# Constant tiles multiplied on TensorE in its waits between the stages of an encoder layer

## The chip, the cores and the metric
One core of one Trainium2 chip. The metric is the device time of one execution in microseconds (us); lower is better. TensorE is the matrix engine, VectorE, ScalarE and GpSimd compute on rows, SyncE issues DMAs.

## The reference
One encoder layer on 1536 tokens (a prompt of 512 and a sample of 1024) of width 1024, in f32:
```
h    = rmsnorm(x, g_mix);  proj = h @ w_in              # 1024 -> 2496 columns
ret  = retention_bidir(rope(q), rope(k), v)              # 8 heads of 64, chunks of 128
mla  = latent_attention(cq, ckv, kr)                     # 4 heads, ranks 256 and 128
x    = x + concat(gated ret, mla) @ w_out
h    = rmsnorm(x, g_ffn)                                 # router: 4 groups x 8 experts,
y    = sum over top-2 of gate * (silu(h@w_g[e]) * (h@w_u[e])) @ w_d[e]
out  = rmsnorm(x + y, g_final)
```
Each expert (32 of them) has three matrices of 1024x512 in f32, 6 MB.

## The kernel before
It runs as stages, each with its own instruction stream per engine; semaphores order the engines. A large product is made by `three_passes` (lines 94 to 98): operands are split into a high and a low part of type fp32r, and hi x hi, hi x lo and lo x hi are added in PSUM. Router, transposes and a few small products are plain f32.

**Projection** (`phase_project`, TensorE from line 338). The loop over 12 token tiles runs twice: V and K first, then Q, C (the latent part) and G, with scores and outputs of the retention between them. At its end TensorE does `turn(N - 2)`, `outputs(N - 1)`, then `turn(N - 1)`: four transposes that wait for GpSimd's gated row (line 320). ScalarE copies the result (line 591), GpSimd stores it (line 324), and the stage ends in a barrier of all engines, after which the semaphores are cleared (lines 105 to 107).

**Attention** (`phase_latent`, TensorE from line 1258). Weights are absorbed first: 8 groups of three 128x128 products into `pt`, after `w_lo` of VectorE (line 1582). Then comes a wait for the constants `s_const` (identity and rotary angles, both loaded by SyncE, lines 1051 and 1053), then `values(0)` (four transposes, waiting for GpSimd's `key_lo` of four tiles, line 1090), `values(1)`, `rotary`, `queries`, and a loop over 48 units of 128 query rows. The last `weigh_last(1)` goes to ScalarE (line 1382) and to memory, and the stage ends in a barrier.

**Mixing and routing** (`phase_mix`, TensorE from line 1870). `project(t, half)` makes 48 matmuls of 128x512 for one tile. For tile t, TensorE issues in this order: `project(t + 1)`, `match_places(t - 2)`, a wait for `x2` (VectorE line 2026), 8 transposes (line 1906), `place_in_queue(t - 1)` (lines 1887 and 1888), a wait for ScalarE's copies of the transposes (line 1942), and the router's 8 matmuls of 36 columns (line 1915). VectorE takes `x2`, the reciprocal root (line 2028), the normalised row (line 2030), the queue steps of the tile before (`queue`, lines 1984 to 2018; the first is line 1988), and the choice of experts (lines 2037 to 2060). In the last tile (`last`), ScalarE does its two copies ahead of the square root (lines 1949 to 1952). After the loop: `match_places(10)`, `place_in_queue(11)`, `match_places(11)`, then the matmul that counts rows per expert (line 1925). VectorE's last steps write `ex.first` (line 2068), the list of the rows of expert 0; it then splits two weight pieces (line 2070).

**Experts** (`phase_experts`, TensorE from line 2322), in the same block, so without a barrier. GpSimd gathers the rows of expert 0 (line 2221) by `ex.first`. TensorE waits for them, transposes them (line 2326), ScalarE and VectorE split them into `xT_hi` and `xT_lo` (line 2472), and `take_in` and `give_out` make the expert's products. Weights come as six pieces of 1 MB per expert into six buffers; a piece is loaded when VectorE has split the one before in its buffer (`s_wlo`, lines 1716 and 2165). VectorE's first expert step is `rows_lo(0)`, two splits and `count_blocks`. All engines execute their instructions in program order.

Of the kernel before, what the change touches and what calls it, by code (L numbers as in the profile page):

```python
# [28 lines left out]
P = 128  # L29
# [64 lines left out]
def three_passes(pe, out, st_hi, st_lo, mv_hi, mv_lo, first, last):  # L94

    pe.matmul(out, st_hi, mv_hi, start=first, stop=False)  # L96
    pe.matmul(out, st_hi, mv_lo, start=False, stop=False)  # L97
    return pe.matmul(out, st_lo, mv_hi, start=False, stop=last)  # L98


def phase_sems(nc, ctx):
# [16 lines left out]
def phase_project(nc, x_all, w_in, g_mix, g_q, g_kv, rope, ident_d, log_decay, gn_g, dist_d, index_d, span_d, mid, mixT, w_cat, absorb, shared):  # L118
    with ExitStack() as ctx:
# [30 lines left out]
        ident = sb("ident", [P, P])  # L150
# [187 lines left out]
        def _(pe):  # L338
# [69 lines left out]
            def turn(t):  # L408
                pe.wait_ge(s_ret, t + 1)
                pe.wait_ge(s_ctev, min(t + 2, N))  # L410
                if t == N - 1:
                    pe.wait_ge(s_rtev, t)
                for j in range(4):
                    ins = pe.transpose(pT[:, j * P:(j + 1) * P], o_sb[:, j * P:(j + 1) * P], ident[:])
                ins.then_inc(s_rt, 1)
# [81 lines left out]
                turn_latent(t)  # L497
            turn(N - 2)
            outputs(N - 1)
            turn(N - 1)  # L500

        @block.scalar
        def _(act):
# [420 lines left out]
def out_piece(shared, table, k, c):  # L924

    first = table[k][c] * 512
    return shared[:, first:first + 512]


def phase_latent(nc, mid, w_cat, w_out, rope, ident_d, mixT, absorb, shared):  # L930

    SCALE = float(NOPE + ROPE) ** -0.5
    with ExitStack() as ctx:
# [8 lines left out]
        ident = sb("ident", [P, P])  # L942
# [151 lines left out]
        def _(pe):  # L1094
# [153 lines left out]
            def aside(u):  # L1248
# [6 lines left out]
                elif u == 44:  # L1255
                    fold(3, 1)

            pe.wait_ge(s_wlo, 1)
            for h in range(HM):
                for k in range(2):  # L1260
# [4 lines left out]
                if h % 2 == 1:  # L1265
                    ins.then_inc(s_m, 1)
            pe.wait_ge(s_const, 32)
            values(0)
            values(1)
            rotary(0)  # L1270
# [9 lines left out]
            for u in range(NU):  # L1280
# [12 lines left out]
                if u == NU - 2:  # L1293
                    weigh_last(0)
            weigh_last(1)

        @block.scalar
        def _(act):
# [421 lines left out]
def phase_mix(nc, block, sems, shared, split, plain, acc, ex, mixT, x_all, g_ffn, w_rg, w_re, ident_d, route_d, blocks_d, x_mid,  # L1720
              h_rows, table, s_tick, s_tock, w_exp):
    with ExitStack() as ctx:
# [43 lines left out]
        pt = acc[:, 2048:3072]  # L1766
# [101 lines left out]
        @block.tensor  # L1868
        def _(pe):
            def project(t, half):  # L1870
                pe.wait_ge(s_mlo, t + 1)
                pe.wait_ge(s_x2, t - 1 if not isinstance(t, int) else max(0, t - 1))
                for b in range(2):
                    for k in range(KD):
                        rows = slice(k * P, (k + 1) * P)
                        ins = three_passes(pe, po[half][:, b * 512:(b + 1) * 512], mT_hi[:, half, rows],
                                           mT_lo[:, half, rows], out_piece(shared, OUT_HI, k, b),
                                           out_piece(shared, OUT_LO, k, b), k == 0, k == KD - 1)
                ins.then_inc(s_po, 1)

            project(0, 0)
            pe.wait_ge(s_const, 112)

            def place_in_queue(t):

                pe.wait_ge(s_hot, t + 1)
                pe.matmul(pp[:, 0:NE], before, hot[:, 2, :], start=True, stop=False)
                pe.matmul(pp[:, 0:NE], ones, seen[:], start=False, stop=True).then_inc(s_pp, 1)

            def match_places(t):  # L1890

                pe.wait_ge(s_match, t + 1)
                pe.matmul(pp[:, 64:65], match[:], row_id[:], start=True, stop=True).then_inc(s_matched, 1)

            def tile(r, half, last):
                t = 2 * r + half
                if not last:
                    project(t + 1, 1 - half)
                if not (isinstance(r, int) and r == 0):
                    match_places(t - 2)  # L1900
                pe.wait_ge(s_x2, t + 1)
                pe.wait_ge(s_htev, 2 * t)
                for b in range(2):
                    for j in range(4):
                        k = 4 * b + j
                        ins = pe.transpose(pt[:, k * P:(k + 1) * P], x2[:, half, k:D:KD], ident[:])  # L1906
                    ins.then_inc(s_ht, 1)
                if not (isinstance(t, int) and t == 0):
                    place_in_queue(t - 1)
                pe.wait_ge(s_htev, 2 * t + 2)  # L1910
                pe.wait_ge(s_rev, t)
                if isinstance(t, int) and t == 0:
                    pe.wait_ge(s_wr, 1)
                for k in range(KD):
                    ins = pe.matmul(pr[:, 0:NG + NE], hT[:, k * P:(k + 1) * P], w_r[:, k, :],  # L1915
                                    start=k == 0, stop=k == KD - 1)
                ins.then_inc(s_r, 1)

            pairs(pe, TILES, tile)
            match_places(TILES - 2)  # L1920
            place_in_queue(TILES - 1)
            match_places(TILES - 1)
            pe.wait_ge(s_spot, TILES + 1)
            pe.wait_ge(ex.s_first, 1)
            pe.matmul(pp[:, 0:NE], ones, seen[:], start=True, stop=True).then_inc(s_count, 1)
# [174 lines left out]
def phase_experts(nc, block, sems, split, plain, acc, ex, w_exp, h_rows, table, s_tick, x_mid, g_final, out, s_normed, count_blocks,  # L2100
# [4 lines left out]
    with ExitStack() as ctx:  # L2105
# [216 lines left out]
        def _(pe):  # L2322
# [30 lines left out]
            def turn_hidden(n):  # L2353
# [3 lines left out]
                    ins = pe.transpose(ph[:, k * P:(k + 1) * P], h_sb[:, k:FE:KF], ident[:])  # L2357
                ins.then_inc(s_ht, 1)

            pe.wait_ge(s_xg[0], 16)  # L2360
            transpose_rows(0, 0)
            transpose_rows(1, 0)

            def step(r, half, final):
                n = 2 * r + half
# [283 lines left out]
```

## Time and profile before

| | us |
|---|---|
| median of 3 runs | 1635.18 (1634.63 to 1635.73) |
| the profiled execution, its own time | 1637.01 |
| its span, first to last instruction | 1635.5 |
| busy: TensorE / VectorE / ScalarE / GpSimd | 1488.1 / 1102.0 / 876.5 / 283.6 |
| mean granted TensorE clock | 0.957 of full |

The profile's page shows busy time by engine and the span in 40 slices of 41 us, with the granted TensorE clock of each. The trace behind it has every instruction with its start, its duration and what ended the idle time before it. Tables of stretches give, after the length, busy us and number of records of TensorE's matmuls, TensorE's weight loads, VectorE, ScalarE and GpSimd, then the granted clock, the DMA engines' busy share and GB/s. A granted clock of 1.00 is 2.4 GHz and 0.50 is 1.2 GHz. A matmul's duration holds its way through the array and overlaps the next; what a row of matmuls costs is the distance between starts.

### The profile page before, as it was taken

To read this page: it belongs to the slowest core of one execution; us is meant where nothing else is said; L and a number is where in the kernel's file an instruction comes from. 1 tells how busy PE (TensorE), PEld (TensorE's weight loads), DVE (VectorE), ACT (ScalarE), POOL (GpSimd) and SP (SyncE) were. 2 spreads that over 40 slices of the span, in tenths; PEclk is the share of its full clock that TensorE was granted. 3 is DMA by queue.
4 is the path that set the end of the run, shared out by engine and by line. 5 is a ranking of instruction groups with operands and counts; after the bars stand their busy time and mean duration, and the time that the engine had idled before them with its cause. 6 is when DMAs were issued, how large, how long until landed. Compare 5 with 4: busy or idle time off the path is not lost.

```text
span 1635.5 us, 21860 instructions
## 1 busy us (share of the span) xinstructions
PE 1488.1 (91%) x7520; PEld 1246.9 (76%) x7520; DVE 1102.0 (67%) x1649; ACT 876.5 (54%) x1150; POOL 283.6 (17%) x270
## 2 busy tenths in 40 slices
PE   6999999999994889998799985999999999999992
PEld 5888888888884677777688874878887878788771
DVE  5655765344343666666256657988888888888886
ACT  6434433233233554554243444867777777777764
POOL 0000111111112300000012123432122212123341
PEclk9999999999996899999899986999999999999996
DMA  7222421221112110001653425999999999999997
GB/s 244 71 95 95 142 69 59 85 71 59 52 39 86 39 59 20 26 29 37 217 215 134 154 80 191 368 377 376 386 381 384 382 366 383 384 384 383 378 346 268
DMA packets 79175, 323.62 MB, mean 198 GB/s; under 512 B 13574, under 2 KB 23814, under 8 KB 54530
## 3 DMA queue, kind: packets, MB, share of 16 engines
q1 hardware_dynamic: 62418, 274.63, 44.7%
q0 software_dynamic: 16688, 48.10, 9.6%
q8 instruction: 40, 0.66, 0.2%
q14 instruction: 29, 0.24, 0.0%
HBM read 279.62 MB, written 51.80 MB: 203 GB/s over the span
## 4 chain that ended last, share of the span: by engine, by line
DMA 19%; PE 13%; DVE 10%; issue 5%; ACT 3%; POOL 1%; ACTq 0%; DVEq 0%; SPq 0%; POOLq 0%
DMA plain<-in_w_down 17%; DVE split L1716 7%; PE acc L96 4%; PE acc L98 4%; PE acc L97 4%; DMA plain<-s_h_rows,plain 1%; PE acc L1915 1%; ACT split L2418 1%; ACT shared L1710 1%; PE acc L1906 1%; DVE plain L2528 1%; DVE shared L1716 0%; POOL s_x_mid L2230 0%; ACT plain L1942 0%; PE acc L2326 0%
## 5 line engine op out<-in xcount | busy, mean ns | idle before, releaser
L1710 ACT CAST shared<-plain 128x2048 fp32r<-128x2048 f32 x192 | 364.8, 1914 | 99.5 <-DMA plain<-in_w_up 67.5
L96 PE MATMUL acc<-shared,split 128*128 128x512 f32 x960 | 386.1, 402 | 20.3 <-DVE split L1969 9.7
L98 PE MATMUL acc<-shared,split 128*128 128x512 f32 x960 | 378.9, 395 | 0.0
L1716 DVE TENSOR_TENSOR split<-plain,shared 128x2048 fp32r<-128x2048 f32 x128 | 287.3, 2285 | 0.0
L96 PEld LDWEIGHTS acc<-shared,split 128*128 128x128 f32 x960 | 183.7, 191 | 58.6 <-DVE split L1969 9.9
L98 PEld LDWEIGHTS acc<-shared,split 128*128 128x128 f32 x960 | 182.9, 190 | 39.6
L97 PE MATMUL acc<-split 128*128 128x512 f32 x512 | 200.7, 392 | 0.0
L96 PE MATMUL a_p<-shared,a_xT_hi 128*128 128x512 f32 (+1 forms) x480 | 194.8, 406 | 3.3 <-DVE a_w_lo L690 3.3
L98 PE MATMUL a_p<-shared,a_xT_lo 128*128 128x512 f32 (+1 forms) x480 | 187.3, 390 | 0.0
L97 PE MATMUL acc<-shared,split 128*128 128x512 f32 x448 | 177.7, 397 | 0.0
L1716 DVE TENSOR_TENSOR shared<-plain,shared 128x2048 fp32r<-128x2048 f32 x64 | 146.0, 2282 | 4.0 <-ACT shared L1710 4.0
L2230 POOL DMA_INDIRECT s_x_mid<-plain x30 | 56.2, 1873 | 384.1 <-DVE plain L2479 379.2
L97 PEld LDWEIGHTS acc<-split 128*128 128x128 f32 x512 | 97.2, 190 | 18.4
L97 PE MATMUL a_p<-a_w_lo,a_xT_hi 128*128 128x512 f32 (+1 forms) x288 | 110.8, 385 | 0.0
L96 PEld LDWEIGHTS a_p<-shared,a_xT_hi 128*128 128x128 f32 x480 | 91.4, 190 | 20.2 <-DVE a_xT_lo L684 3.7
L98 PEld LDWEIGHTS a_p<-shared,a_xT_lo 128*128 128x128 f32 x480 | 91.1, 190 | 18.0
L97 PEld LDWEIGHTS acc<-shared,split 128*128 128x128 f32 x448 | 86.4, 193 | 18.1
L1374 ACT CAST c_pT_hi<-c_pt 128x512 fp32r<-128x512 f32 x80 | 45.2, 589 | 76.2 <-PE c_pt L1207 76.1
L2221 POOL DMA_INDIRECT plain<-s_h_rows,plain x32 | 78.0, 2437 | 19.9 <-PE acc L2326 6.5
L97 PE MATMUL a_p<-shared,a_xT_hi 128*128 128x512 f32 x192 | 75.5, 393 | 0.0
L802 DVE TENSOR_TENSOR a_late<-a_p,a_dmat 128x512 f32<-128x512 f32 x24 | 16.6, 691 | 85.1 <-PE a_p L388 85.1
L1545 DVE TENSOR_TENSOR c_pT_lo<-c_pt,c_pT_hi 128x512 fp32r<-128x512 f32 x80 | 52.7, 684 | 22.9 <-ACT c_pT_hi L1374 22.9
(349 smaller groups left out, 2617.1 us busy)
## 6 DMA issues: line engine op xcount, KB each, us to landing
plain<-in_w_gate SPq DMA_DIRECT2D x64, 1024.0 KB, 11.1
plain<-in_w_up SPq DMA_DIRECT2D x64, 1024.0 KB
plain<-in_w_down SPq DMA_DIRECT2D x64, 1024.0 KB, 10.8
a_x_sb<-in_x SPq DMA_DIRECT2D x24, 512.0 KB, 4.2
s_mid<-a_kv SPq DMA_DIRECT2D x12, 512.0 KB, 2.9
a_kv<-s_mid SPq DMA_DIRECT2D x12, 512.0 KB, 3.5
plain<-s_mixT SPq DMA_DIRECT2D x12, 512.0 KB, 5.4
plain<-in_x SPq DMA_DIRECT2D x12, 512.0 KB, 4.0
```

The costliest lines, as they stand in the source:

```text
L96: pe.matmul(out, st_hi, mv_hi, start=first, stop=False)
L97: pe.matmul(out, st_hi, mv_lo, start=False, stop=False)
L98: return pe.matmul(out, st_lo, mv_hi, start=False, stop=last)
L802: nc.vector.tensor_tensor(sc[:, odd].rearrange("p a i -> p (a i)"), pS[:], dmat[:, odd].rearrange("p a i -> p (a i)"), ALU.mult).then_inc( ...
L1374: nc.scalar.copy(pT3_hi[:, 4 * i:4 * i + 4, j * P:(j + 1) * P], pt[:, c * 512:(c + 1) * 512].rearrange("p (k i) -> p k i", k=4)).then_inc( ...
L1545: nc.vector.tensor_tensor(pT3_lo[:, 4 * i:4 * i + 4, j * P:(j + 1) * P], pt[:, c * 512:(c + 1) * 512].rearrange("p (k i) -> p k i", k=4), ...
L1710: eng.copy(self.w_hi[j // 2][:, cols], self.source(j, moved)).then_inc(self.s_whi[j], 1)
L1716: eng.tensor_tensor(self.w_lo[j // 2][:, cols], self.source(j, moved), self.w_hi[j // 2][:, cols].bitcast(F32), ALU.subtract).then_inc(sel ...
L1906: ins = pe.transpose(pt[:, k * P:(k + 1) * P], x2[:, half, k:D:KD], ident[:])
L1915: ins = pe.matmul(pr[:, 0:NG + NE], hT[:, k * P:(k + 1) * P], w_r[:, k, :], start=k == 0, stop=k == KD - 1)
L2221: pool.indirect_dma_start(out=xg[half][:], out_offset=None, in_=h_rows, in_offset=bass.IndirectOffsetOnAxis(ap=index, axis=0), bounds_chec ...
L2230: pool.indirect_dma_start(out=x_rows, out_offset=bass.IndirectOffsetOnAxis(ap=index, axis=0), in_=y_sb[half][:], in_offset=None, bounds_ch ...
```

## The change
A helper issues `times` matmuls of a constant tile by a constant tile into a PSUM region that nobody reads before it is overwritten. It is called at twelve places of TensorE's stream: 102 matmuls of 128x512 fp32r (16, 28, 12, 12, 14 and 20) and 140 of the f32 identity by itself, 128x128 (36, 32, 6, 7, 52 and 7). No wait is added or removed, and no other engine's stream is changed.
```diff
--- before.py
+++ after.py
@@ -96,6 +96,12 @@
     pe.matmul(out, st_hi, mv_hi, start=first, stop=False)
     pe.matmul(out, st_hi, mv_lo, start=False, stop=False)
     return pe.matmul(out, st_lo, mv_hi, start=False, stop=last)
+
+
+def keep_warm(pe, out, weights, moving, times):
+
+    for _ in range(times):
+        pe.matmul(out, weights, moving, start=True, stop=True)
 
 
 def phase_sems(nc, ctx):
@@ -497,7 +503,10 @@
                 turn_latent(t)
             turn(N - 2)
             outputs(N - 1)
+            spare = w_lo[0][:, 2, :]
+            keep_warm(pe, bank[0][:], spare[:, 0:P], spare, 16)
             turn(N - 1)
+            keep_warm(pe, bank[0][:], spare[:, 0:P], spare, 28)
 
         @block.scalar
         def _(act):
@@ -1255,6 +1264,8 @@
                 elif u == 44:
                     fold(3, 1)
 
+            spare = shared[:, 13312:13824]
+            keep_warm(pe, pt[:, 0:512], spare[:, 0:P], spare, 12)
             pe.wait_ge(s_wlo, 1)
             for h in range(HM):
                 for k in range(2):
@@ -1265,6 +1276,7 @@
                 if h % 2 == 1:
                     ins.then_inc(s_m, 1)
             pe.wait_ge(s_const, 32)
+            keep_warm(pe, ps[0][:, 0:512], spare[:, 0:P], spare, 12)
             values(0)
             values(1)
             rotary(0)
@@ -1293,6 +1305,8 @@
                 if u == NU - 2:
                     weigh_last(0)
             weigh_last(1)
+            spare = v_hi[:, 0:4, :].rearrange("p t d -> p (t d)")
+            keep_warm(pe, ps[0][:, 0:512], spare[:, 0:P], spare, 14)
 
         @block.scalar
         def _(act):
@@ -1878,6 +1892,8 @@
                                            out_piece(shared, OUT_LO, k, b), k == 0, k == KD - 1)
                 ins.then_inc(s_po, 1)
 
+            spare = out_piece(shared, OUT_HI, 0, 0)
+            keep_warm(pe, po[1][:, 0:512], spare[:, 0:P], spare, 20)
             project(0, 0)
             pe.wait_ge(s_const, 112)
 
@@ -1898,6 +1914,8 @@
                     project(t + 1, 1 - half)
                 if not (isinstance(r, int) and r == 0):
                     match_places(t - 2)
+                if last:
+                    keep_warm(pe, po[0][:, 0:P], ident[:], ident[:], 36)
                 pe.wait_ge(s_x2, t + 1)
                 pe.wait_ge(s_htev, 2 * t)
                 for b in range(2):
@@ -1918,8 +1936,11 @@
 
             pairs(pe, TILES, tile)
             match_places(TILES - 2)
+            keep_warm(pe, po[0][:, 0:P], ident[:], ident[:], 32)
             place_in_queue(TILES - 1)
+            keep_warm(pe, po[0][:, 0:P], ident[:], ident[:], 6)
             match_places(TILES - 1)
+            keep_warm(pe, po[0][:, 0:P], ident[:], ident[:], 7)
             pe.wait_ge(s_spot, TILES + 1)
             pe.wait_ge(ex.s_first, 1)
             pe.matmul(pp[:, 0:NE], ones, seen[:], start=True, stop=True).then_inc(s_count, 1)
@@ -2357,9 +2378,11 @@
                     ins = pe.transpose(ph[:, k * P:(k + 1) * P], h_sb[:, k:FE:KF], ident[:])
                 ins.then_inc(s_ht, 1)
 
+            keep_warm(pe, py[:, 0:P], ident[:], ident[:], 52)
             pe.wait_ge(s_xg[0], 16)
             transpose_rows(0, 0)
             transpose_rows(1, 0)
+            keep_warm(pe, py[:, 0:P], ident[:], ident[:], 7)
 
             def step(r, half, final):
                 n = 2 * r + half
```

## Rows read from the trace of the kernel before

**Rows 1.** The page: busy time and record count of each engine; granted clock by slices.
```profile
PE 1488.1 (91%) x7520; PEld 1246.9 (76%) x7520; DVE 1102.0 (67%) x1649; ACT 876.5 (54%) x1150; POOL 283.6 (17%) x270
...
PEclk9999999999996899999899986999999999999996
```

**Rows 2.** Table of stretches (from:to, length; each engine busy us and records; clock; DMA).
```profile
480.00:490.60 10.60, 9.83 (x69) 8.46 (x68) 2.38 (x4) 3.06 (x4) 3.49 (x3) 1.00 0.14 51
...
494.00:521.00 27.00, 10.84 (x47) 10.00 (x48) 6.70 (x8) 7.43 (x15) 8.72 (x14) 0.50 0.43 129
...
507.70:512.90 5.20, 5.14 (x24) 5.14 (x24) 1.73 (x4) 3.58 (x9) 4.12 (x7) 0.50 1.04 296
...
784.00:794.00 10.00, 3.90 (x9) 3.13 (x10) 1.23 (x1) 1.04 (x1) 1.95 (x8) 0.50 0.80 237
...
968.80:971.60 2.80, 0.01 (x1) 0.00 (x0) 2.02 (x14) 0.00 (x0) 1.57 (x2) 1.00 0.01 0
...
971.90:1005.70 33.80, 15.07 (x55) 13.15 (x56) 21.13 (x70) 15.23 (x16) 9.30 (x10) 0.50 0.37 126
...
974.00:980.30 6.30, 6.25 (x28) 6.02 (x28) 1.92 (x7) 5.18 (x7) 0.57 (x1) 0.50 0.21 83
...
1040.00:1560.00 520.00, 506.28 (x2355) 416.94 (x2354) 458.52 (x309) 385.89 (x308) 144.36 (x94) 1.00 1.01 380
```

**Rows 3.** Timeline of TensorE, 477 to 520 us (start, us; bracket: idle before).
```profile
495.44 1.12 PE L414 MATMUL a_p<-a_ident,a_late 128*128 128x128 f32 x4 [4.60 <-POOL a_late L320]
...
516.66 1.09 PE L1108 MATMUL c_po<-c_ident,c_key_hi 128*128 128x128 f32 x4 [3.52 <-POOL c_key_lo L1090]
```

**Rows 4.** Timeline of TensorE, start of the mixing.
```profile
790.10 0.79 PE L96 MATMUL acc<-shared,split 128*128 128x512 f32 x1 [9.69 <-DVE split L1969]
```

**Rows 5.** Timeline of TensorE, 952 to 1020 us, the routing tail.
```profile
966.64 1.98 PE L1915 MATMUL acc<-plain 128*128 128x36 f32 x16 [0.35 <-ACT plain L1942]
...
968.45 0.36 PE L1893 MATMUL acc<-plain 128*128 128x1 f32 x2
...
974.05 1.97 PE L1906 MATMUL acc<-plain 128*128 128x128 f32 x8 [5.24 <-DVE plain L2026]
...
980.72 0.58 PE L1893 MATMUL acc<-plain 128*128 128x1 f32 x2 [0.39 <-DVE plain L1997]
...
986.09 0.63 PE L1887 MATMUL acc<-plain 128*128 128x32 f32 x2 [4.79 <-DVE plain L2058]
...
988.23 0.59 PE L1893 MATMUL acc<-plain 128*128 128x1 f32 x2 [1.08 <-DVE plain L1997]
...
998.35 1.97 PE L2326 MATMUL acc<-plain 128*128 128x128 f32 x8 [7.58 <-DMA plain<-s_h_rows,plain]
...
1001.72 0.79 PE L96 MATMUL acc<-shared,split 128*128 128x512 f32 x1 [1.40 <-DVE split L2472]
```

**Rows 6.** Timeline of TensorE at 480 us.
```profile
479.60 0.39 PE L97 MATMUL a_p<-shared,a_xT_hi 128*128 128x512 f32 x1
479.83 0.39 PE L98 MATMUL a_p<-shared,a_xT_lo 128*128 128x512 f32 x1
480.15 1.16 PE L388 MATMUL a_p<-a_qd,a_kv 64*128 64x128 f32 x8
```

**Rows 7.** Groups of TensorE by line and shape: the router's matmul.
```profile
L1915 PE MATMUL acc<-plain 128*128 128x36 f32 x192 | 25.4, 291 | 4.2 <-ACT plain L1942 4.2
```

**Rows 8.** Instructions of line 119: duration min/median/max ns, start us.
```profile
L119 POOLq DRAIN  x1: 2997/2997/2997, 500.0 to 500.0; - x1
```

**Rows 9.** Timeline of SyncE at 506 us, and DMA issues there (last: us to landing).
```profile
506.45 0.57 SPq L1053 DMA_DIRECT2D c_angles<-in_rope  x1
...
c_angles<-in_rope SPq DMA_DIRECT2D x1, 768.0 KB, 7.1
```

**Rows 10.** Timeline of VectorE in the tail.
```profile
978.28 0.17 DVE L2028 RECIPROCAL plain<-plain 128x1 f32<-128x1 f32 x1 [4.29 <-ACT plain L1952]
...
987.19 0.16 DVE L1988 COPY plain<-acc 128x1 f32<-128x1 f32 x1 [0.95 <-PE acc L1888]
```

## The prediction

> **What bounds the kernel now.** First the page: TensorE is busy for 91% of the span, and its granted clock is high except in a few slices; every matmul record has a weight load of its own, 7520 against 7520 [rows 1]. Then the table of stretches, which gives the clock level and the records of each: three stretches at 1.2 GHz (clock 0.50) matter, 494.0 to 521.0, 784.0 to 794.0 and 971.9 to 1005.7; from 1040 to 1560 the DMA engines are full and TensorE has 506 of 520 us of work [rows 2]. So the end is set by one thread: projection, attention and mixing on TensorE and its partners, then the routing tail (967 to 1002), then weights that stream at the DMA limit. The stream begins when the expert stage begins, so a microsecond won or lost before 1002 reaches the end nearly whole. The waits that the change fills are 4.6 us before the last turn of the projection, the barrier after it, 3.5 us before values(0) [rows 3], 9.7 us ahead of the mixing [rows 4], and in the tail 5.2, 4.8, 1.1 and 7.6 us [rows 5]. Each ends on another engine or a DMA: if the filler is longer than the wait, TensorE is what is late.
>
> **Prices.** The change adds 102 matmuls of 128x512 fp32r and 140 of ident by ident, plain f32. The first kind starts every 0.23 us at the high clock (479.60 to 479.83) [rows 6], and costs 0.43 at the low one (9 records in 3.90) [rows 2]. The second is the point. A plain f32 matmul leaves two records: the router has 8 matmuls in each of 12 tiles and shows 192 [rows 7]. Sixteen such records run from 966.64 to 968.45, 0.113 each [rows 5]; with 128 moving columns, as ident has, eight take 1.16 us, start-up and last end included, 0.145 each [rows 6]. I take 0.112 a record, 0.224 a matmul, since the second figure holds both ends. At the low clock 24 records of 128x128 take 5.14 us, 0.213 each [rows 2], so 0.427 a matmul. Identical weights one after another would not be loaded once only: loads equal matmuls everywhere [rows 1].
>
> The Trainium skill, page "TensorE: Matmul & The Clock Gate", section "Back-to-back issue gap", gives about 81 ns for a sustained matmul of 128 columns with its load. By that figure alone (an estimate) 36 would take 2.9 us and 52 would take 4.2 us, and all fillers would fit.
>
> **End of the projection.** 16 matmuls are 3.6 us of a 4.6 us wait; the turn then runs at the high clock and its 1.12 us [rows 3] shrink by about 0.45. It is on the path (ScalarE copy, store, barrier): -0.45. The 28 behind it are 6.4 us, done near 502.5. GpSimd is in a drain of 3.0 us from 500.0 to 503.0 ahead of the barrier [rows 8], which hides them: 0, but with 0.1 us to spare, and were that cover gone they would cost up to 2 us.
>
> **Start of attention.** 12 matmuls (2.7 us) fit between the barrier at 504 and the products of the absorbed weights at 507.7 [rows 2], and those 24 go faster, to no use: values(0) at 516.66 waits for GpSimd's key_lo, not for them [rows 3]. The next 12 stand behind a wait for the constants, which includes the angles: issued 506.45, 7.1 us to landing, so 513.5 [rows 9]. From the products' end near 510 to 513 TensorE idles 3 us; in this kernel 2.8 us (968.8 to 971.6) without work is followed by the low clock [rows 2]. So they probably begin low and end between 515.8 (all high, hidden) and 518.2 (all low, values(0) 1.5 late); I take 0.6 late. The clock is then high from values(0) on instead of from 521: what ran 516.66 to 521.0 at half speed takes about 2.3 us less, less 0.4 where ScalarE's eviction decides. Sum: -1.3 (between -2.3 and 0). A later wait of this stage that the change does not fill may drop the clock as now or at another moment: 0, up to 1.5 either way.
>
> **Start of the mixing.** 14 (3.2 us) behind the last weighing end by 783.6, before the barrier; 20 (4.5 us) from 784.5 end by 789.1, before the first projection at 790.10 [rows 4]. That one then runs 9 matmuls at 0.23 instead of 0.43: -1.9. Nothing hides it: the tiles of the mixing follow on TensorE one behind the other. In all the front gives -0.45 - 1.3 - 1.9 = -3.6; the level may dip elsewhere too, once the work has moved (a tile of the mixing dips when its router work falls badly), so I take -3.2, between -6 and 0.
>
> **The routing tail**, times as before, the front's gain left out. (a) 36 ident matmuls are queued at 968.67, ahead of the wait for x2: 72 x 0.112 = 8.05, to 976.7, where the transposes had started at 974.05 [rows 5]. Behind them are ScalarE's two copies and its square root, then VectorE's reciprocal at 978.28, 4.23 after the transposes' start [rows 10]; fast transposes make that about 3.35, so 980.05: +1.8. (b) match_places(10) moves to 982.5. Before it lies the router's 36-column work and a wait of 2 us, much like what preceded 971.9, so I hold the clock to be low again near here. Then 32 matmuls: 64 x 0.213 = 13.7, to 996.6, where place_in_queue(11) wanted to start at 986.09 + 1.8 = 987.9. VectorE's next step, 1.10 behind it (986.09, 987.19) [rows 5, 10], comes at 997.6: +10.4. (c) 6 matmuls, 2.6 us, fill a wait that is 1.1: with the delay so far +10.7. (d) ex.first and the gather follow, rows landing at 998.35 + 10.7 = 1009.05; 7 and then 52 matmuls, 14 and 104 records, 25.2 us with the count's matmul between, hold TensorE until 1026.0: +27.7. (e) 7 more after the transposes, 3.0 us, against a wait of 1.4 (1000.3 to 1001.72): +29.0. VectorE's splits of weights and the count of blocks stand behind xT_lo, and the buffers that free the next loads behind those; so VectorE, TensorE and the stream all start late. Nothing there can move forward. Total +29.0 - 3.2 = +25.8.
>
> Why the fillers should not bring the clock back themselves: the 24 records of 128x128 at 507.7 to 512.9 had 5.14 of 5.2 us and stayed at 1.2 GHz; so did the 28 records of 974.0 to 980.3 (6.25 of 6.3 us) [rows 2]. These are the rows nearest to ident by ident. What did raise it were 512-column records, after 3.9 us of them from 790.10 [rows 2, 4].
>
> The skill's page says the reverse as advice (section "Why this matters for your kernels": keep TensorE busy continuously to reach and hold the high clock). By that rule the second rival below comes out. Its section "Part 4: PE-mode transpose" says that transposes do not bring the full clock; 974.0 to 980.3 agrees.
>
> The profiled execution took 1637.01 us (span 1635.5), so the sum is 1662.8 in its terms; the median of the runs is 1.83 lower: **1661.0 us**.
>
> **Rivals.** A, forecast: clock low from (b) to the experts: 1661, and 1655 to 1670 with its unknowns (drop late in (b): -3; the front; and if (a) already falls low, 36 x 0.427 = 15.4 instead of 8.05: +7.4). Chance 0.62.
> B, the ident matmuls hold or raise the clock. For: the fillers leave little idle, and short f32 records at the high level kept it (480.0 to 490.6 is at 1.00 throughout [rows 2]). Against: the two stretches above. All high: (a) +1.8, (b) 989.9 against 987.9 and less 0.5 for the faster pair: +3.3, 52 x 0.224 = 11.6 puts the transposes at 1005.5, +7.2; the faster transposes and first expert products give back 2.8: about +4.4 on TensorE, but VectorE's chain begins +6.4 late and is full to 1040. So +6.4 - 3.2 = +3.2, 1638.4; with one low spell of 16 records, 2 us more, 1640.4. Chance 0.28.
> C, the other side: faster. If ident by ident costs one record, the 36 take 4.0 us of 5.2, the 52 take 5.8 of 7.6, nothing is late and all is high: tail -0.3 - 0.5 - 0.8 - 1.9 = -3.5, sum -6.8, 1628.4. It decides at 0.146 us a matmul (5.24/36; 7.58/52). For: the counts fill three quarters of each wait at 0.112. Against: two records in every f32 matmul. Chance 0.06.
> D, the clock does what B says and the front gives its full 6: 1634 to 1637, chance 0.04.
>
> **Numbers.** The likeliest case gives 1661. The range must reach into B: 1637 to 1670 leaves out C, D and the far end of A, under 2 in 10; A's own is 1655 to 1670. About 0.2% (3.3 us) is what a measurement of this kernel can tell from no change. Faster by more, C: 0.08 with a strong front. Within: B's lower half and D: 0.12. Slower: 0.80.
>
> **What would show it.** The page: 382 more matmul records (102 + 280). Table of stretches: 784 to 814 at 1.00 and 516 to 521 mostly so; in the tail 0.50 from about 982 to the experts, ident records 0.213 apart, the 52 taking 22 us, and idle time of TensorE before place_in_queue(11) and the first gather's transposes gone, with VectorE waiting for TensorE instead. If those records are 0.11 apart, B is right; if there are 140 of them, C. If the transposes do not start late at (a), the sum fails at its first step.

## The result, and the profile after

The changed kernel is slower: 1645.97 us median (8 runs, 1642.03 to 1652.84) against 1637.72 (8 runs, 1634.63 to 1641.85) of the kernel before beside it, ratio 1.0047, interval 1.003 to 1.0063. The forecast was 1661.0. The profiled execution took 1646.24 us (span 1644.7), 9.2 more than the 1637.01 of before. In the changed kernel the filler's line is L104, L388 to L420 of before are 6 lines further down, and L1887 to L1925 have become L1903 to L1946.

The page, answering to [rows 1]:
```profile
PE 1536.8 (93%) x7902; PEld 1290.4 (78%) x7902; DVE 1101.5 (67%) x1649; ACT 875.8 (53%) x1150; POOL 289.4 (18%) x270
...
PEclk9999999999999999999999999999999999999996
```
382 more matmul records, so ident by ident does leave two records each. The three dents of the clock line before (68, 8 and 86) are gone, and the time goes up all the same.

Table of stretches of the changed kernel (columns as in [rows 2]; the third from the end is the granted clock):
```profile
512.00:517.00 5.00, 4.69 (x15) 3.63 (x16) 0.70 (x2) 1.21 (x3) 2.38 (x5) 0.66 0.29 100
517.00:521.00 4.00, 3.67 (x26) 3.22 (x25) 1.86 (x4) 0.58 (x1) 0.00 (x0) 1.00 0.24 66
784.00:794.00 10.00, 9.20 (x41) 7.25 (x40) 1.23 (x1) 1.05 (x1) 1.17 (x6) 1.00 0.78 236
969.70:974.10 4.40, 4.40 (x26) 4.40 (x26) 3.48 (x22) 0.14 (x1) 2.01 (x2) 0.61 0.01 0
...
985.70:991.00 5.30, 5.30 (x26) 5.30 (x27) 4.06 (x26) 0.18 (x2) 2.15 (x3) 0.50 0.51 179
991.00:999.30 8.30, 8.30 (x76) 8.30 (x75) 2.90 (x20) 7.22 (x5) 0.00 (x0) 0.99 0.00 0
999.30:1011.00 11.70, 11.70 (x107) 11.70 (x107) 4.02 (x3) 0.00 (x0) 5.01 (x3) 1.00 0.57 207
...
1040.00:1560.00 520.00, 506.61 (x2367) 417.32 (x2366) 459.51 (x309) 390.05 (x311) 146.27 (x91) 1.00 1.01 381
```
The rows of the tail decide. The 72 records of the first group begin at 969.7. The first eight start 0.11 us apart, at the high level, then come sixteen 0.21 apart (0.61 over 969.7 to 974.1), then 0.11 again: the clock fell and rose inside one unbroken group. From 985.7 to 991 TensorE works through ident by ident at 0.50, and from 991 on, still in the same 64 records, at 0.99: here the clock rose inside the fillers. From 999.3 to 1011 there is nothing but fillers, at 1.00. And the stream from 1040 to 1560 is as it was, so what the tail loses stays lost.

Timeline of TensorE in the routing tail, answering to [rows 5]:
```profile
969.51 0.36 PE L1909 MATMUL acc<-plain 128*128 128x1 f32 x2
969.74 9.91 PE L104 MATMUL acc<-plain 128*128 128x128 f32 x72
979.49 1.04 PE L1924 MATMUL acc<-plain 128*128 128x128 f32 x8
...
985.27 0.58 PE L1909 MATMUL acc<-plain 128*128 128x1 f32 x2 [2.05 <-DVE plain L2018]
985.72 9.96 PE L104 MATMUL acc<-plain 128*128 128x128 f32 x64
995.52 0.31 PE L1903 MATMUL acc<-plain 128*128 128x32 f32 x2
...
999.28 11.86 PE L104 MATMUL acc<-plain 128*128 128x128 f32 x104
1010.97 1.04 PE L2347 MATMUL acc<-plain 128*128 128x128 f32 x8
```
Each group is longer than the wait that it fills (5.2, 4.8 and 7.6 us before). The steps behind the fillers have no bracket any more: nothing outside TensorE holds them up. VectorE now waits for TensorE instead. Timeline of VectorE, answering to [rows 10] (the reciprocal, and the first step behind place_in_queue(11)):
```profile
982.84 0.16 DVE L2049 RECIPROCAL plain<-plain 128x1 f32<-128x1 f32 x1 [7.78 <-ACT plain L1973]
...
996.09 0.16 DVE L2009 COPY plain<-acc 128x1 f32<-128x1 f32 x1 [5.30 <-PE acc L1904]
```
Timeline of TensorE at the two front places, answering to [rows 3, 4]:
```profile
494.51 0.66 PE L420 MATMUL a_p<-a_ident,a_late 128*128 128x128 f32 x4 [0.89 <-POOL a_late L326]
494.93 6.63 PE L104 MATMUL a_p<-shared 128*128 128x512 f32 x28
...
512.31 4.61 PE L104 MATMUL c_ps<-shared 128*128 128x512 f32 x12 [3.04 <-DMA c_angles<-in_rope]
516.75 0.60 PE L1117 MATMUL c_po<-c_ident,c_key_hi 128*128 128x128 f32 x4
...
783.25 4.78 PE L104 MATMUL acc<-shared 128*128 128x512 f32 x20 [1.00 <-PEq L113]
788.83 0.50 PE L96 MATMUL acc<-shared,split 128*128 128x512 f32 x1 [0.80 <-DVE split L1990]
```

Where the 9.2 us come from, as differences of the same instruction's start in the two traces, each counted from the first transpose of its execution:

| instruction | change minus before, us |
|---|---|
| VectorE's x2 of tile 0 of the mixing | -3.24 |
| x2 of tile 11 | +1.02 |
| first transpose of tile 11 | +5.39 |
| place_in_queue(11) | +9.38 |
| `ex.first` | +8.85 |
| first transpose of the first gathered rows | +12.57 |
| transposes of the second gather | +10.57 |
| end | +9.19 |

Not all of the first row is the fillers' doing. The last turn of the projection, whose start is set by GpSimd and not by a filler, already stands 0.98 us earlier (495.44 less 4.94 for the first transpose before, 494.51 less 4.99 after), and so does VectorE's work from 200 us on, long before the first filler. So the front's fillers bring 2.3 us, the mixing takes 4.3, the tail costs 11.55, and 2.0 of that come back because the experts' first products run at 2.4 GHz.

The mixing was in no step of the change. Its stretch 800 to 965, before, then the change:
```profile
800.00:965.00 165.00, 161.11 (x839) 137.46 (x838) 91.96 (x374) 65.20 (x94) 30.68 (x40) 0.98 0.46 166
```
```profile
800.00:965.00 165.00, 159.98 (x818) 136.22 (x817) 91.92 (x374) 65.10 (x94) 30.10 (x39) 0.96 0.46 166
```
The clock drops for a few microseconds on single tiles, twice before and four times here. Each of the 41 drops of this stretch in the fifteen profiles of this case begins inside the router's 36-column matmuls or within 1.1 us of the start of their last record. A drop costs 1.3 to 1.7 us, most 1.6 (steps in the distances between the x2 of neighbouring tiles). Only one of before's two cost anything: tile 2 took 16.65 us with its drop, and 16.60 without one in the run with fp32r fillers in the tail.

### The profile page after: what moved, and what is told of

It reads as the page before. It is cut to its first block, busy times and chain, and to the rows that moved or that the text cites. A ratio compares the mean times of both kernels' runs of the same rounds, so it can differ in the third digit from the quotient of the medians.

```text
span 1644.7 us, 22623 instructions
## 1 busy us (share of the span) xinstructions
PE 1536.8 (93%) x7902; PEld 1290.4 (78%) x7902; DVE 1101.5 (67%) x1649; ACT 875.8 (53%) x1150; POOL 289.4 (18%) x270
## 4 chain that ended last, share of the span: by engine, by line
DMA 21%; PE 13%; DVE 10%; issue 5%; ACT 3%; SPq 0%; ACTq 0%; DVEq 0%; POOLq 0%; POOL 0%
DMA plain<-in_w_down 18%; DVE split L1730 8%; PE acc L96 3%; PE acc L98 3%; PE acc L97 3%; PE acc L104 2%; DMA plain<-s_mixT 1%; PE acc L1933 1%; ACT split L2441 1%; ACT shared L1724 1%; DVE plain L2551 1%; DMA s_x_mid<-plain 1%; PE acc L1924 1%; ACT plain L1963 0%; DMA plain<-s_x_mid 0%
## 5 line engine op out<-in xcount | busy, mean ns | idle before, releaser
L2242 POOL DMA_INDIRECT plain<-s_h_rows,plain x32 | 85.6, 2673 | 24.6 <-DVE plain L2089 9.9
```

The source lines that it names most:

```text
L2242: pool.indirect_dma_start(out=xg[half][:], out_offset=None, in_=h_rows, in_offset=bass.IndirectOffsetOnAxis(ap=index, axis=0), bounds_chec ...
```

## The experiments

Differences "at x2 of tile 0", "at x2 of tile 11", "at the gathered rows" and "at the end" are measured as in the table above. They hold what the execution had won or lost before the first filler: at the projection's last turn the profiles of the runs stand between -0.62 and +2.59 us. The kernel before took 1639.37 us (32 runs), 1638.52 (23 runs), 1639.14 (23 runs) and 1639.16 (7 runs) beside the four groups of runs.

**Front alone.** All ident calls left out:
```diff
-                    keep_warm(pe, po[0][:, 0:P], ident[:], ident[:], 36)
...
-            keep_warm(pe, py[:, 0:P], ident[:], ident[:], 7)
```


> Edit: the six fillers of identity tiles in the routing tail are left out; the six of 128x512 fp32r stay. Theory Q (queue): the loss comes from identity tiles that are queued ahead of real work and outlast the waits, 2 records of 0.11 us each. Then this kernel keeps the front's gain (the first x2 of the mixing 3.2 us earlier than before) and has the tail of before: 3 us faster than before, ratio 0.998, less what low spells in the mixing tiles take. Rival L (level): the loss comes from moving the work against the clock's low spells, which fall on mixing tiles (4.3 us given back there in the changed kernel). Then this kernel is no faster than before, 1.000 to 1.001, with four low spells in the mixing.


Measured: 1642.39 us, ratio 1.0011 (0.9996 to 1.0025). In its profile x2 of tile 0 stands at -2.2 us (0.4 of that from before the first filler) and tile 11 at +1.0: 3.2 us go in the mixing. One of its two drops, from 830.6 to 837.4, lasts twice as long as the others. The time is what rival L gave, with two drops and not four.

**Tail alone.** The six fp32r calls left out:
```diff
-            keep_warm(pe, bank[0][:], spare[:, 0:P], spare, 16)
...
-            keep_warm(pe, po[1][:, 0:512], spare[:, 0:P], spare, 20)
```


> Edit: only the six fillers of identity tiles in the routing tail, none of the six of 128x512. Theory Q: the transposes of expert 0's rows start 11 us later than before and the experts' later blocks 9 to 10 us, ratio 1.006. Rival L: 1.000 to 1.002, since nothing ahead of the tail has moved.


Measured: 1646.9 us, ratio 1.0046 (1.0029 to 1.0064). The ident fillers carry the whole slowdown. From x2 of tile 11 to the gathered rows the tail is 11.0 us longer (expected 11; the change: 11.55), and 2.7 come back before the second gather.

**Half the ident counts**, front kept:
```diff
-                    keep_warm(pe, po[0][:, 0:P], ident[:], ident[:], 36)
+                    keep_warm(pe, po[0][:, 0:P], ident[:], ident[:], 18)
...
-            keep_warm(pe, py[:, 0:P], ident[:], ident[:], 52)
+            keep_warm(pe, py[:, 0:P], ident[:], ident[:], 26)
```
(32 became 16, 6 and both 7 became 3.)


> Edit: as the change, but the identity fillers halved: 18, 16, 3, 3, 26 and 3, so that at 0.224 us a tile each ends before its wait does (4.0 of 5.2, 3.6 of 4.8, 0.7 of 1.1, 5.8 of 7.6). Theory Q: no delay in the tail, the transposes of expert 0's rows about 1 us early and the first expert products 2 us shorter, so 3 to 6 us faster than before, ratio 0.997. If the clock falls in the tail in spite of them, the 26 tiles take 11 us at the low level and come 3 us late: about 1.000. Rival L: 1.000 to 1.003, as the change nearly.


Measured: 1637.81 us, ratio 0.9999 (0.9979 to 1.0018). x2 of tile 11 to the gathered rows: -0.2 against before. At two records a matmul, counts of half the size fit into the waits, as the 0.224 us of a matmul say (18 x 0.224 = 4.0 of 5.2; 26 x 0.224 = 5.8 of 7.6), and 1.9 us come back in the experts' first products. The 3 to 6 us that theory Q expected did not come: this profile stands at +0.1 at tile 0, and, with two drops, at +2.1 at tile 11.

**Only the 52 halved:**
```diff
-            keep_warm(pe, py[:, 0:P], ident[:], ident[:], 52)
+            keep_warm(pe, py[:, 0:P], ident[:], ident[:], 26)
```


> Edit: the change with 26 identity tiles instead of 52 ahead of the wait for expert 0's rows. Theory Q: the rows land near 1007.3 in the changed kernel's time while the 52 tiles end at 1011.0, so this one is 3.7 us faster than the changed kernel, ratio to before 1.0025. Rival (the gather is what is late, and the tiles are hidden beside it): as the changed kernel, 1.005.


Measured: 1647.36 us, ratio 1.0044 (1.0025 to 1.0064). Timeline of TensorE at this place:
```profile
1000.53 6.05 PE L104 MATMUL acc<-plain 128*128 128x128 f32 x52
1008.42 1.51 PE L2347 MATMUL acc<-plain 128*128 128x128 f32 x8 [1.83 <-DMA plain<-s_h_rows,plain]
```
The wait for the gather is back: 26 end before the rows land, so in the change 52 made TensorE 12.57 - 8.85 = 3.7 us late. The runs' median does not show these 3.7 us: it lies between the 1.0025 of theory Q and the 1.005 of its rival. In this profile the clock dropped five times in the mixing and x2 of tile 11 stands at +4.2, which hides them (from there to the gathered rows it is 5.8 us, against 11.55); whether that holds for all 12 runs (1637.82 to 1653.8) is not shown.

**512-column fillers in every tile of the mixing**, none of the change's:
```diff
                 if not (isinstance(t, int) and t == 0):
                     place_in_queue(t - 1)
+                keep_warm(pe, po[half][:, 0:512], spare[:, 0:P], spare, 2)
                 pe.wait_ge(s_htev, 2 * t + 2)
```


> The kernel before, with none of the change's fillers, and 2 fillers of 128x512 fp32r in each of the 12 tiles of the mixing, between the pair of place_in_queue of the tile before and TensorE's wait for s_htev. So far the mixing showed 2, 4, 2, 6, 2 and 6 spells at the low clock in the profiled executions of six kernels. Theory L (those spells set how far the front's gain is given back, about 1.7 us each): with 512-column records in TensorE's wait of each tile the spells between 815 and 960 vanish, the mixing's last tile ends 2 to 4 us earlier than in the kernel before's profile, ratio about 0.998. Rival (the fillers outlast the wait in each tile, or the router's work alone lets the clock fall): as many spells as before, mixing 0 to 5 us longer, ratio 1.000 to 1.003.


Measured: 1637.21 us, ratio 0.999 (0.9977 to 1.0004). The same stretch of its trace:
```profile
800.00:965.00 165.00, 163.64 (x872) 139.04 (x870) 92.21 (x377) 66.18 (x96) 30.69 (x40) 1.00 0.46 169
```
The drops are gone, and x2 of tile 11 moves from +0.20 at tile 0 to -1.70: 1.9 us, just under the 2 to 4 expected, since only one of before's two drops had cost anything. The drops went as theory L said; by the interval the ratio may be a gain or none. Of the 1.7 us, 0.5 reach the end (-0.48): time won ahead of the experts doesn't arrive whole.

**Both corrected:** counts 16, 24, 12, 0, 14, 20 in front, 18, 16, 3, 3, 26, 3 in the tail, and the two fillers in each tile of the mixing.


> The change with its fp32r fillers but for the 12 ahead of values(0), with ident counts 18, 16, 3, 3, 26, 3 in place of 36, 32, 6, 7, 52, 7, and the 2 fillers in each tile of the mixing. If the front is worth 2 to 3 us at the first tile of the mixing, the mixing's spells are gone, and the tail is no longer than before with fast first expert products (-1.9 in the half-count kernel), the sum is -4 to -7 us: ratio 0.996 to 0.998. If the mixing's spells stay or the fillers there cost what they save: as the half-count kernel, 0.999 to 1.000.


Measured: 1634.24 us, ratio 0.9965 (0.995 to 0.9979): faster than both kernels. Timeline of TensorE at the first gather, and the mixing:
```profile
990.80 6.05 PE L104 MATMUL acc<-plain 128*128 128x128 f32 x52
998.78 1.29 PE L2348 MATMUL acc<-plain 128*128 128x128 f32 x8 [1.93 <-DMA plain<-s_h_rows,plain]
```
```profile
800.00:965.00 165.00, 163.33 (x849) 138.49 (x848) 92.54 (x375) 65.08 (x94) 30.21 (x39) 0.98 0.46 168
```
The ratio came as expected, the path only in part. In this profile (end at -4.16) one drop is left in the mixing in spite of the fillers, 832.4 to 839.2, as long as two, so tile 11 stands at +1.14 after -0.62 at tile 0 (and that after +2.59 before the first filler). The tail then gives 0.9, the experts' first products 1.7, the rest up to the last gather 0.7, and 2.0 come behind the last gather, where nothing was changed; their cause was not followed.

**The same without the fillers in the mixing**
```diff
-                keep_warm(pe, po[half][:, 0:512], spare[:, 0:P], spare, 2)
```


> The best version so far without its two fillers in each tile of the mixing: what do these bring in it? Theory L (spells at the low clock on the mixing's tiles take back the front's gain): 2 to 6 spells instead of 1, ratio 0.998 to 1.000. Rival (the gain of the best version comes from leaving out the 12 before values(0) and from the halved tail): one or two spells all the same, ratio 0.996 to 0.997.


Measured: 1638.41 us, ratio 0.9989 (0.9965 to 1.0013), 12 runs from 1628.27 to 1646.61; with the fillers the 12 runs lay between 1627.49 and 1636.72. Four drops in this profile. The spread of the runs falls from 18 to 9 us with the fillers, as it should if the drops are behind it. What each run has on record is its mean granted clock, and that goes with the time: without the fillers 1628.27 us at 0.978 and 1646.61 at 0.967. So the spread is time at the low clock; that it is the mixing's was seen in profiles of different kernels only. The two kernels were run in different groups (23 runs each of the kernel before beside them spread over 10 and 13 us), and the intervals of the two ratios meet, so the medians alone don't prove a gain.

**The same without the ident fillers** (both corrected, tail as before)
```diff
-                    keep_warm(pe, po[0][:, 0:P], ident[:], ident[:], 18)
...
-            keep_warm(pe, py[:, 0:P], ident[:], ident[:], 3)
```


> The best version so far without ident by ident in the tail, the front's and the mixing's fillers kept. The halved ident groups left the path of the tail unchanged (-0.2 to +0.3) and gave back 1.7 to 1.9 us in the experts' first products. So: ratio 0.997 to 0.998, about 2 us over the best version; if the tail's fillers bring nothing, 0.9965 like it.


Measured: 1637.12 us, ratio 0.9984 (0.9968 to 1.0). Between this ratio and that of both corrected lie 3 us for the halved ident groups, but the two intervals meet. The profiles say why it isn't sure: from x2 of tile 11 to the second gather the three kernels with halved groups stand at -2.1, -2.6 and +0.5 (the last without the mixing's fillers; its clock is low again from 1008.5 to 1015.3), this one at +1.0. A gain of the tail's fillers is likely and not shown.

**Does a long row of 128-column records raise the clock?** Kernel before, 40 fp32r matmuls of 128x128 behind the barrier of the attention:
```diff
+            keep_warm(pe, pt[:, 0:P], spare[:, 0:P], spare[:, 0:P], 40)
             pe.wait_ge(s_wlo, 1)
```


> The kernel before with 40 matmuls of 128x128 fp32r at the start of the attention, behind the barrier, where the clock is low and 24 records of that size follow. It asks why ident by ident raised the clock in the routing tail and these 24 did not. Theory 'run' (any unbroken run of 128-column records raises it, the 24 were only too few): the clock rises within the 40, records 0.213 apart at first and about half of that later. Theory 'kind' (plain f32 does it, fp32r of 128 columns does not): all 64 records at 0.213, 13.6 us, clock 0.50 throughout, values(0) about 4 us late or more.


Measured: 1639.06 us (one run). Table of stretches:
```profile
504.40:517.90 13.50, 13.41 (x63) 13.44 (x64) 5.08 (x5) 5.78 (x12) 3.85 (x8) 0.50 0.67 200
```
64 weight loads and their matmuls without a gap, and 0.50 throughout: "run" is refuted, for fp32r of 128 columns. x2 of tile 0 stands at +4.0, as expected.

**Plain f32 of 64 columns** in the same place:
```diff
+            keep_warm(pe, pt[:, 0:64], spare[:, 0:P].bitcast(F32), spare[:, 0:64].bitcast(F32), 20)
```


> The kernel before with 20 plain f32 matmuls of 64 columns (40 records) at the start of the attention, at the low clock. It asks whether plain f32 records raise the clock at half the columns too. If the kind decides: the clock rises during them, records about 0.21 apart at first, then about half. If columns decide: it stays at 0.50, records at one spacing throughout.


Measured: 1650.62 us (one run; its mixing had 6 drops and lost 6.3 us). Table of stretches, and the group of fillers:
```profile
505.00:518.80 13.80, 13.72 (x64) 13.53 (x64) 5.08 (x5) 5.63 (x13) 4.39 (x9) 0.50 0.66 195
```
```profile
L104 PE MATMUL c_pt<-shared 128*128 128x64 f32 x40 | 8.8, 422 | 7.7 <-PEq L113 7.7
```
It stays low too, though these records are plain f32. The 40 take 8.77 us, as did the 40 fp32r records of 128 columns in the run before. Columns are not the only difference from ident by ident in the tail: the place is another too, and plain f32 of 128 columns was not run at this place, nor of 64 in the tail.

**The tail's fillers as fp32r.** The change, with the first four ident groups replaced by as many records of fp32r:
```diff
-                    keep_warm(pe, po[0][:, 0:P], ident[:], ident[:], 36)
+                    keep_warm(pe, po[0][:, 0:P], mT_hi[:, 1, 0:P], mT_hi[:, 1, 0:P], 72)
...
-            keep_warm(pe, po[0][:, 0:P], ident[:], ident[:], 32)
+            keep_warm(pe, po[0][:, 0:P], mT_hi[:, 1, 0:P], mT_hi[:, 1, 0:P], 64)
```


> The change, with its first four groups of ident by ident in the routing tail (36, 32, 6 and 7 plain f32 matmuls, two records each) replaced by 72, 64, 12 and 14 fp32r matmuls of 128x128: as many records, as wide and with the same spacing, of the other kind. The 52 and the 7 behind them stay. Theory 'kind' (unbroken 128-column records of plain f32 raise the clock, fp32r ones of 128 columns do not; 64 of these stayed at 0.50 in the run with 40 added): the prediction's case A comes out up to the first gather: once low in (a) or (b) the clock stays low, the 64 take 13.6 us instead of 9.96, place_in_queue(11) starts 4 to 11 us later than with the change and the end comes 4 to 12 us later, 1650 to 1659. Theory 'run' (the tail raises it for a reason of its place, whatever the kind): low spells of some 3.4 us as with the change, time within 2 us of the change's, 1646.


Measured: 1657.38 us, ratio 1.013 (1.0085 to 1.0176). Timeline of TensorE, then two stretches:
```profile
964.87 13.75 PE L104 MATMUL acc<-split 128*128 128x128 f32 x72
978.42 1.94 PE L1924 MATMUL acc<-plain 128*128 128x128 f32 x8
...
985.50 13.89 PE L104 MATMUL acc<-split 128*128 128x128 f32 x64
999.20 0.57 PE L1903 MATMUL acc<-plain 128*128 128x32 f32 x2
...
1006.41 14.18 PE L104 MATMUL acc<-plain 128*128 128x128 f32 x104
```
```profile
966.80:1005.00 38.20, 37.81 (x179) 37.55 (x178) 14.01 (x69) 12.79 (x13) 5.04 (x7) 0.50 0.12 43
1006.40:1020.40 14.00, 14.00 (x105) 14.00 (x106) 1.34 (x2) 0.00 (x0) 4.72 (x6) 0.83 0.53 183
```
For 38 us TensorE is busy 99% of the time with fp32r and small work, at 0.50. Then come the 104 records of ident by ident that this kernel kept, and the clock rises inside them (0.83 over the group). The 64 take 13.89 us, where the prediction had 13.7. From x2 of tile 11 (-3.84) to the gathered rows (+22.03) it costs 25.9 us. That is close to the 27.7 of the prediction's case A, by other terms: here the first group was low too (13.75 us, not 8.05), and the 104 records behind were low only at their start (14.18, not 22.2).

**Plain f32 on the same numbers.** The last run changed kind and values together (ident is nearly all zero); this one changes the values alone:
```diff
-                    keep_warm(pe, po[0][:, 0:P], ident[:], ident[:], 36)
+                    keep_warm(pe, po[0][:, 0:P], mT_hi[:, 1, 0:P].bitcast(F32), mT_hi[:, 1, 0:P].bitcast(F32), 36)
```
(and so for the 32, 6 and 7.)


> The change, with its first four groups of ident by ident in the routing tail kept as plain f32 and in number (36, 32, 6, 7), but reading the tile of the mixed rows that the run with fp32r read, instead of ident, whose elements are nearly all zero. The run with fp32r changed the kind and the data together; this one changes the data alone. If the kind decides: the clock rises inside the 36 or the 32 as with the change, time as the change, 1643 to 1650. If the data decide (numbers that are not zero hold the clock down): the clock stays low through the groups as in the fp32r run, 1652 to 1660.


Measured: 1650.97 us, ratio 1.0074 (1.0046 to 1.0102), whose interval meets the change's. Timeline of TensorE:
```profile
971.73 8.28 PE L104 MATMUL acc<-split 128*128 128x128 f32 x72
...
986.08 9.60 PE L104 MATMUL acc<-split 128*128 128x128 f32 x64
```
The 64 start low and end high as with ident: between this run and the last, the kind of the records makes the difference in the trace, and not their values. The median lies just outside both expectations (1643 to 1650 and 1652 to 1660), with four runs; the profiled one took 1644.88. The 72 ran at the high level from end to end and show what (a) costs then: 8.28 us, transposes 2.7 later than x2 asks.

**The 36 alone**, kernel before otherwise.
```diff
             match_places(t - 2)
+                if last:
+                    keep_warm(pe, po[0][:, 0:P], ident[:], ident[:], 36)
```


> The kernel before with the 36 ident by ident ahead of the wait for x2 alone. With the change this group took 9.91 us, one low spell inside it, and delayed the transposes of the last tile by 4.4 us. If the group alone does that: transposes +2.8 (all high) to +4.5, place_in_queue(11) +2 to +4, the gathered rows about as much, and the end as much less nothing, since the clock is low again long before the experts: 1640 to 1642 in the profiled run. If its delay is absorbed by the waits behind it: under +1 at the gathered rows.


Measured: 1643.28 us (one run). 9.91 us again, transposes +6.29 with x2 of tile 11 at +1.93 (so +4.4), the gathered rows +5.34 (so +3.4), the end +6.0. The delay isn't absorbed; about 1 us comes back as faster transposes. The time is over the 1640 to 1642 expected, since 1.9 us were lost ahead of the group, with two drops in the mixing that cost 1.6 us each.

## Why the prediction was wrong

**The sign and the places were right, the size was not.** Predicted +25.8 us of the profiled execution, measured +9.2.

The step that failed is the one headed "Why the fillers should not bring the clock back themselves", and with it the 0.213 us a record in (b), (d) and (e). It took 24 records of fp32r and 28 of transposes and 36 columns [rows 2] as the rows nearest to ident by ident. The runs with fp32r fillers and with plain f32 on real numbers show that the first is not near: 64 fp32r records without a gap stay at 1.2 GHz, 64 and 104 plain f32 records of the same width and spacing don't. With fp32r in the first four groups the kernel took 1657 us, near the forecast, but its terms were others than A's (13.75, 13.89 and 14.18 us for the three large groups, where A had 8.05, 13.7 and 22.2), so that agreement is partly luck.

Step by step, in the profiled execution:
- Prices: two records a matmul, right (382 more). 0.112 a record at the high level, right (104 in 11.7 us). Low 0.213, right for as long as it was low.
- End of the projection: 0.46 faster turn, right (0.66 against 1.12); the 28 end at 501.6, hidden.
- Start of attention: the 12 began high, but the clock fell after the first four of them (starts 0.23, then 0.43 us apart), and they took 4.61. Counted from the projection's last turn, values(0) is 1.0 us late; predicted 0.15 (-0.45 + 0.6). At the start of the mixing's first product the execution stands at -1.32, which is -0.3 from that turn; predicted -1.75. So the attention gave nothing in this profile, where 1.3 had been taken.
- Start of the mixing: -1.9, measured -3.24 + 1.32 = -1.92.
- The front as a whole: -3.2 taken, -3.24 measured at x2 of tile 0. That agreement is luck: 0.98 of it was there before the first filler. From the projection's last turn to x2 of tile 0 it is -2.3 here, and -2.9, -2.1, -1.7, -1.2 and +0.4 in five other profiles of the same front code. At x2 of tile 11 it stands at +1.02. "The level may dip elsewhere too" was the right sentence with the wrong price: +4.3, not +0.4. In the runs the front alone is worth nothing that can be measured.
- (a) predicted 8.05 us, +2.65 at the transposes and +1.8 at the reciprocal; measured 9.91, +4.4 and +3.5. The level was high at its start, as taken, but fell 0.9 us into the group, behind the router's 36-column work and eight filler records, and rose again inside it. All high, it was 8.28 in the run on real numbers.
- (b) 64 records in 9.96, predicted 13.7: low for its first 5 us, then high. place_in_queue(11) stands 8.4 behind x2, predicted 10.5; nearer than its terms, since 1.7 too little from (a) stands against 3.8 too much in the 64.
- (c) to (e): `ex.first` 7.8 behind x2, predicted 10.7. The 52 take 11.9 and not 22.2, so the gathered rows are 11.55 late, not 27.7, and the first products, fast, give back 2.0.
- The sum: -1.0 before the first filler, -2.3 from the front's fillers, +4.3 in the mixing, +11.55 and -2.0 in the tail, -1.4 in the experts (not followed) = +9.2.

So the case that came is nearest to B. Its sum, 1640.4 with one low spell, allowed for 16 low records; the changed kernel's trace has about 16 in (a) and 24 in (b) (at 0.1 us more each, 4 us), and the front's gain did not last. The Trainium skill, page "TensorE: Matmul & The Clock Gate", section "Why this matters for your kernels", advises to keep TensorE continuously busy to reach the high clock. Inside the 64 records the trace agrees (0.50, then 0.99). It doesn't inside the 72, where the clock fell with TensorE at work without a gap, nor in the runs with fp32r of 128 columns (0.50 over 38.2 us, 99% busy), and there the measurement decides. By the same page's section "Back-to-back issue gap" (81 ns for a matmul of 128 columns) 52 would take 4.2 us, an estimate; the trace has 11.86, since plain f32 leaves two records of 0.112 each.

**Open.** Why the clock rose inside one kind of record and not inside another is not shown, only where: it rose inside unbroken groups of plain f32 of 128 columns and in products of 512 columns, and stayed low through fp32r of 128 columns (in two places) and through 40 plain f32 records of 64 (one run, one place). x2 of tile 0 stands at -0.6, +1.8 and -2.9 in the three profiles of a front without the 12 ahead of values(0). Part of that lies ahead of all fillers (+2.6, +1.3 and -0.2 at the projection's last turn); from there it is -3.2, +0.5 and -2.7, and the rest is open. The 12 do delay values(0): from that turn it is 1.0 to 3.5 us late in the six profiles with them, and between 0.6 early and 0.3 late in the three without. At tile 0 the two sets overlap, so whether the 12 cost anything in the end is open too.

## What to carry to other kernels

A filler is a price times a count against one measured wait: take the price per matmul from records of the same type and width (plain f32 is two records), and leave room for a low spell. Filling a wait too full costs more than the clock it saves: halving the counts turned +0.47% into -0.01%. With two wide records in each iteration of the loop as well, where the clock drops behind short work, and without the 12 ahead of values(0), it was -0.35%. Look where time saved ahead of a loop goes, before counting it, and compare two traces at a place ahead of the change first: here they were 0.98 us apart there.

## What had not been expected of the hardware

TensorE was busy 99% of 38.2 us and stayed at 1.2 GHz (179 records, nearly all fp32r of 128 columns or narrower work), while the clock rose within one group of plain f32 of the same width and the same spacing. It also fell 0.9 us into such a group, with no gap in the work. A plain f32 record of 64 columns starts every 0.21 us at the low clock, as one of fp32r and 128 does (40 in 8.8 us). And the drops in the mixing fall on other tiles in other profiles: 1 to 6 of them in the twelve profiles without fillers there, 0, 1 and 1 in the three with. One kernel's times spread by 10 us and more (before: 1633.96 to 1644.23 in 23 runs), the slower runs at the lower mean granted clock (0.952 at 1644.23, 0.957 at 1633.96).
